# Mixer end of a two-layer hybrid block: the gate half of the last input chunk, the activation tables and the order of the output projection are rearranged

## The reference, cut to what matters

```
proj = h @ w_in ; rq, rk, rv, rg, sz, sxbc, sdt, bq, bk, bv = split(proj)
ro = head_groupnorm(retention(rq, rk, rv), w) * silu(rg)          # 256 columns
so = gated_rmsnorm(ssd(conv(sxbc), dt) + D*x, sz, w)               # 512 columns
bo = stick_breaking(bq, bk, bv)                                    # 256 columns
out = concat(ro, so, bo) @ w_out                                   # 1024 x 1024
```

## Time and profile before

| | before |
|---|---|
| median of 3 runs | 1516.62 us |
| lowest, highest | 1515.53, 1518.11 us |
| the profiled execution's own time | 1514.14 us |
| its span | 1512.0 us |
| PE busy | 1487.2 us (98%) |
| DVE busy | 1175.3 us (78%) |
| ACT busy | 981.7 us (65%) |

### The profile page before, as it was taken

One profiled execution on the slowest core, in us unless ns is written; L12 is line 12 of the kernel. 1 busy time (PEld: TensorE's weight loads), 2 busy tenths in 40 slices (PEclk: granted clock), 3 DMA queues, 4 the chain that ended last, 5 costly groups with the idle time before them and its releaser, 6 DMA issues.

```text
span 1512.0 us, 19204 instructions
## 1 busy us (share of the span) xinstructions
PE 1487.2 (98%) x7301; PEld 1237.0 (82%) x7304; DVE 1175.3 (78%) x844; ACT 981.7 (65%) x757; POOL 48.9 (3%) x53
## 2 busy tenths in 40 slices
PE   9999999999999999999999999999999999999997
PEld 7987788888988878888878888887888888888885
DVE  5875544444787698898878888878889888888886
ACT  6574533444556677777777777776777777777774
POOL 1010000000000000002000000200000200000010
PEclk9999999999999999999999999999999999999999
DMA  9625555554552499999989999999999998999992
GB/s 348 217 72 181 188 180 188 193 177 129 195 167 98 148 327 382 375 357 372 372 305 360 373 374 350 376 329 336 373 368 363 366 375 320 363 371 376 350 374 108
DMA packets 190647, 437.71 MB, mean 289 GB/s; under 512 B 9376, under 2 KB 13664, under 8 KB 190448
## 3 DMA queue, kind: packets, MB, share of 16 engines
q1 hardware_dynamic: 188256, 433.91, 80.0%
q0 software_dynamic: 1120, 2.20, 0.6%
q10 hardware_dynamic: 1200, 0.56, 0.1%
HBM read 435.59 MB, written 1.05 MB: 289 GB/s over the span
## 4 chain that ended last, share of the span: by engine, by line
PE 95%; DVE 3%; ACT 1%; issue 1%; DMA 0%; ACTq 0%; SPq 0%; DVEq 0%
PE ps L1316 29%; PE ps L1318 29%; PE ps L1317 29%; PE ps L1611 2%; PE ps L1568 1%; PE ps L1586 1%; PE ps L1587 0%; PE ps L1813 0%; PE ps L1379 0%; PE ps L1378 0%; PE ps L1377 0%; PE ps L1371 0%; DVE w_lo L831 0%; DMA x<-in_x_dram 0%; DVE hm L821 0%
## 5 line engine op out<-in xcount | busy, mean ns | idle before, releaser
L1163 DVE TENSOR_TENSOR w_lo<-raw,w_hi 128x2048 fp32r<-128x2048 f32 x333 | 754.6, 2289 | 122.5 <-ACT w_hi L658 120.0
L658 ACT ACTIVATE w_hi<-raw 128x2048 fp32r<-128x2048 f32 x332 | 630.2, 1919 | 170.5 <-PE ps L1318 170.5
L1316 PE MATMUL ps<-w_hi,aT_hi 128*128 128x512 f32 (+1 forms) x1296 | 511.0, 394 | 8.3 <-issue 3.2
L1318 PE MATMUL ps<-w_hi,aT_lo 128*128 128x512 f32 (+1 forms) x1296 | 503.4, 388 | 0.0
L1317 PE MATMUL ps<-w_lo,aT_hi 128*128 128x512 f32 (+1 forms) x1296 | 502.5, 388 | 0.0
L1316 PEld LDWEIGHTS ps<-w_hi,aT_hi 128*128 128x128 f32 x1296 | 243.4, 188 | 61.8 <-issue 5.9
L1318 PEld LDWEIGHTS ps<-w_hi,aT_lo 128*128 128x128 f32 x1296 | 243.2, 188 | 51.8
L1317 PEld LDWEIGHTS ps<-w_lo,aT_hi 128*128 128x128 f32 x1296 | 243.6, 188 | 48.6
L831 DVE TENSOR_TENSOR w_lo<-raw,w_hi 128x2048 fp32r<-128x2048 f32 (+2 forms) x81 | 176.7, 2186 | 101.8 <-ACT w_hi L478 101.6
L478 ACT ACTIVATE w_hi<-raw 128x2048 fp32r<-128x2048 f32 (+2 forms) x81 | 148.2, 1830 | 106.8 <-PE ps L1318 105.7
L1316 PE MATMUL ps<-w_hi,s2T_hi 128*128 128x512 f32 x544 | 213.1, 392 | 0.0
(11 more groups left out here) (274 smaller groups left out, 910.9 us busy)
## 6 DMA issues: line engine op xcount, KB each, us to landing
raw<-in_moe_w_gate_dram SPq DMA_DIRECT2D x112, 1024.0 KB, 6.9
raw<-in_moe_w_up_dram SPq DMA_DIRECT2D x112, 1024.0 KB, 7.6
raw<-in_moe_w_down_dram SPq DMA_DIRECT2D x112, 1024.0 KB, 7.0
raw<-in_w_in_dram SPq DMA_DIRECT2D x20, 1024.0 KB, 7.1
raw<-in_ffn_w_gate_dram SPq DMA_DIRECT2D x14, 1024.0 KB, 5.1
raw<-in_ffn_w_up_dram SPq DMA_DIRECT2D x14, 1024.0 KB, 5.1
raw<-in_ffn_w_down_dram SPq DMA_DIRECT2D x14, 1024.0 KB, 4.9
raw<-in_w_out_dram SPq DMA_DIRECT2D x8, 1024.0 KB, 5.1
```

The source lines that it names most:

```text
L658: nc.scalar.activation(moe_hi(pos), raw[:, slot, :], ACT.Copy).then_inc(hi_ready, 1)
L1163: V.tensor_tensor(moe_lo(pos), raw[:, pos % 6, :], moe_hi(pos).bitcast(F32), ALU.subtract)\
L1316: mm(out, lhs_hi, rhs_hi, start=start, stop=False, skip_group_check=True)
L1318: return mm(out, lhs_lo, rhs_hi, start=False, stop=stop, skip_group_check=True)
```

## The change

All of it is in the mixer, so it happens twice.

- Chunk 6 is no longer a `win_chunk`. `rvg_part(l, half, part)` multiplies 256 columns: part 0 is rv, for both token blocks into bank 1, and part 1 is rg into bank 0. The value part keeps the places of the two old halves. The gate part of both halves comes after the retention sums, and only it counts `split_used` up.
- ACT preloads one table that holds exp and ln ahead of abs, exp and ln, and again ahead of the last exp. It loads the sqrt table after the copy of rv and the silu table after the two square roots. The silu of rg and the split of piece 15 move behind the square roots, piece 15 first.
- Both `keep_warm` calls go. `mixT(0)` comes ahead of `log_weights`, into bank 3.
- `w_out` takes the steps 2, 3, 0, 1 of the first half, so it can begin with the quarter that `mixT(0)` brings. One block of `w_out(0, 1)` moves ahead of the weighted sums of stick breaking. The second half begins, for token block 0, with the steps 0 and 1 of both its pieces, ahead of the last quarter.
- On DVE the splits of pieces 15 and 16 each move one place forward.

```diff
-MIXT = [1, 0, 5, 4]
+MIXT = [1, 3, 5, 4]
 # ACT
+                nc.scalar.preload_act_table_set("natural_log_exp_and_others")
                 act.wait_ge(sb_z, l + 1)
...
-                chunk_done(6)
-                pv = ps[:, 0:2, :]
-                nc.scalar.activation(rv[:], pv[:, :, 0:256], ACT.Copy).then_inc(rv_ready, 1)
-                nc.scalar.activation(rg[:], pv[:, :, 256:512], ACT.Silu).then_inc(win_out, 1)
-                wout_split(l, 1)
+                both = lambda bank: ps[:, bank, :].rearrange("p (b n) -> p b n", b=NB)
+                act.wait_ge(rv_psum, l + 1)
+                nc.scalar.activation(rv[:], both(1), ACT.Copy).then_inc(rv_ready, 1)
+                sqrt_table()
...
+                nc.scalar.preload_act_table_set("silu_and_others")
+                wout_split(l, 1)
+                chunk_done(6)
+                nc.scalar.activation(rg[:], both(0), ACT.Silu).then_inc(rg_ready, 1)
...
                 mixT(1)
+                nc.scalar.preload_act_table_set("natural_log_exp_and_others")
                 wout_split(l, 2)
 # DVE
+                dve.wait_ge(rg_ready, l + 1)
                 V.tensor_tensor(hm[:, :, 0:256], cvf[:, 0:512].rearrange("p (b n) -> p b n", b=NB), rg[:], ALU.mult)\
...
                 mixT(0)
+                wout_split(l, 1)
                 mixT(1)
 
                 dve.wait_ge(sb_log, l + 1)
                 V.tensor_scalar(xb4, z4, 0.0, None, ALU.min).then_inc(sb_min, 1)
-                wout_split(l, 1)
+                wout_split(l, 2)
                 dve.wait_ge(sb_w, l + 1)
                 V.tensor_tensor(xb4, xb4, strict, ALU.mult).then_inc(sb_wm, 1)
-                wout_split(l, 2)
 # PE
+            def rvg_part(l, half, part):
+
+                g, bank, c0 = MIX_BASE[l] + 12 + half, (1, 0)[part], 256 * part
+                pe.wait_ge(lo_ready[g % 6], g // 6 + 1)
+                hi, lo = win_view(w_hi, g % SPL, 512), win_view(w_lo, g % SPL, 512)
+                for b in range(NB):
+                    for kk in range(4):
+                        k = 4 * half + kk
+                        ins = passes(ps[:, bank, b * 256:(b + 1) * 256], aT_hi[:, 2 * k + b, :], aT_lo[:, 2 * k + b, :],
+                                     hi[:, kk, c0:c0 + 256], lo[:, kk, c0:c0 + 256], start=k == 0 and b == 0,
+                                     stop=k == KD - 1)
+                return ins
...
-                win_chunk(l, 6, (0,))
+                rvg_part(l, 0, 0)
...
-                win_chunk(l, 6, (1,))
+                rvg_part(l, 1, 0).then_inc(rv_psum, 1)
...
                 ins.then_inc(ret_y, 1)
+                for half in range(2):
+                    rvg_part(l, half, 1).then_inc(split_used, 1)
...
+                pe.wait_ge(mix_ssd, l + 1)
+                mixT(0)
                 pe.wait_ge(sb_sp, l + 1)
                 for h in range(BH):
                     ins = log_weights(h)
                 ins.then_inc(sb_log, 1)
-                keep_warm(0, 8)
-                pe.wait_ge(mix_ssd, l + 1)
-                mixT(0)
                 pe.wait_ge(mix_ret, l + 1)
                 mixT(1)
-                keep_warm(2, 6)
+                pe.wait_ge(mixT_lo, 4 * l + 1)
+                w_out(0, 0, steps=(2, 3))
                 pe.wait_ge(mixT_lo, 4 * l + 2)
-                w_out(0, 0)
+                w_out(0, 0, steps=(0, 1))
+                w_out(0, 1, (0,))
                 pe.wait_ge(sb_wm, l + 1)
...
                 mixT(2)
-                w_out(0, 1, (0,))
+                w_out(0, 1, (1,))
                 pe.wait_ge(mix_sb, l + 1)
                 mixT(3)
-                w_out(0, 1, (1,))
+                pe.wait_ge(mixT_lo, 4 * l + 3)
+                w_out(1, 0, (0,), (0, 1))
+                w_out(1, 1, (0,), (0, 1))
                 pe.wait_ge(mixT_lo, 4 * l + 4)
-                w_out(1, 0, (0,))
-                w_out(1, 1, (0,))
-                w_out(1, 0, (1,))
+                w_out(1, 0, (0,), (2, 3))
+                w_out(1, 1, (0,), (2, 3))
+                w_out(1, 0, (1,), range(4))
```

More of the change, by code:

```diff
@@ L895, in mixer @@
                 dve.wait_ge(heads_in[l], 48)
-                dve.wait_ge(win_out, 7 * l + 1)
+                dve.wait_ge(win_out, 6 * l + 1)
                 V.tensor_tensor(sm3(2), sm3(2), bc(heads8[:, l, 0, :].unsqueeze(1), [P, NB, SH]), ALU.add)\
@@ L925, in conv @@
                     dve.wait_ge(conv_tap, taps[0])
-                dve.wait_ge(win_out, 7 * l + 2)
+                dve.wait_ge(win_out, 6 * l + 2)
                 conv(3, range(4))
@@ L933, in mixer @@
                 conv(0, range(4))
-                dve.wait_ge(win_out, 7 * l + 3)
+                dve.wait_ge(win_out, 6 * l + 3)
                 conv(3, range(4, XT))
@@ L939, in mixer @@
                 conv(0, range(4, XT))
-                dve.wait_ge(win_out, 7 * l + 4)
+                dve.wait_ge(win_out, 6 * l + 4)
                 dve.wait_ge(tables_in, 16)
@@ L1323, in win_chunk @@
                 if ci >= 2:
-                    pe.wait_ge(win_out, 7 * l + ci - 1)
+                    pe.wait_ge(win_out, 6 * l + ci - 1)
                 tiles = TILES_T.get(name, 0)
@@ L1425, in mixer @@
                 mm(cT[:, P:T], a3[:, 1], m_le, start=False, stop=True, **opts).then_inc(cs_psum, 1)
-                pe.wait_ge(win_out, 7 * l + 4)
+                pe.wait_ge(win_out, 6 * l + 4)
                 for m in range(4):
@@ L1461, in mixer @@
                 ins.then_inc(ret_psum, 1)
-                win_chunk(l, 6, (0,))
+                pe.wait_ge(win_out, 6 * l + 5)
+                rvg_part(l, 0, 0)
                 pe.wait_ge(s_ret, l + 1)
@@ L1467, in mixer @@
                 ins.then_inc(sb_z, 1)
-                win_chunk(l, 6, (1,))
-                pe.wait_ge(win_out, 7 * l + 6)
+                rvg_part(l, 1, 0).then_inc(rv_psum, 1)
+                pe.wait_ge(win_out, 6 * l + 6)
                 for g in range(SG):
@@ L1501, in mixT, with w_out @@
                     ins.then_inc(mixT_psum, 1)
-                def w_out(half, n, blocks=(0, 1), steps=range(4)):
+                def w_out(half, n, blocks=(0, 1), steps=(2, 3, 0, 1)):
                     g = MIX_BASE[l] + 14 + 2 * half + n
@@ L1510, in w_out @@
                             ins = passes(ps[:, 2 * b + n, :], aT_hi[:, 2 * k + b, :], aT_lo[:, 2 * k + b, :],
-                                         hi[:, kk, :], lo[:, kk, :], start=k == 0, stop=k == KD - 1)
-                        if (half, n, b) == (1, 1, 0):
+                                         hi[:, kk, :], lo[:, kk, :], start=k == 2, stop=k == KD - 1)
+                        if (half, n, b, steps[-1]) == (1, 1, 0, 3):
                             ins.then_inc(mix_block0, 1)
-                    if blocks[-1] == NB - 1 and steps[-1] == 3:
+                    if blocks[-1] == NB - 1 and steps[-1] == (1, 3)[half]:
                         ins.then_inc(split_used, 1)
+                pe.wait_ge(mix_ssd, l + 1)
+                mixT(0)
                 pe.wait_ge(sb_sp, l + 1)
@@ L1548, in mixer @@
                 else:
-                    w_out(1, 1, (1,))
+                    w_out(1, 1, (1,), range(4))
             def gather_fill(p, fill):
```

5 lines of the change are left out of this document (2 added, 3 removed).

## The result

The changed kernel takes 1511.92 us (median of 10 runs, 1508.69 to 1513.58) against 1516.64 us before (10 runs, 1514.19 to 1518.32). The ratio is 0.9965, 95% interval 0.9956 to 0.9974: by this ratio 5.3 us less, between 3.9 and 6.7 (the two medians are 4.7 apart). The forecast was 1510.1, 6.5 us less. The profiled executions took 1510.22 and 1514.14 us, with spans of 1508.1 and 1512.0.

What follows compares the result with a forecast made beforehand. PE was taken to bound the kernel. Per layer 4.76 - 0.75 - 0.10 - 0.65 = 3.26 us, twice 6.5, so 1516.6 - 6.5 = 1510.1 us; forecast's own range 1508.6 to 1511.6, wider range 1506.8 to 1514.0.

Steps and rivals of the forecast that it cites:

- The hole, 4.76 us: At each mixer end, PE's zero matmuls and waits before the first output projection would give way to real work, saving 4.76 us.
- The halved matmuls, +0.75: In the last input chunk, 96 matmuls of 256 columns instead of 48 of 512 would cost PE 0.75 us more per layer.
- The stick weights, +0.10: Ahead of the stick sums, PE would wait 0.1 us per layer for the stick weights, bounds 0 to 0.7.
- the tie: PE would ask for the stick weights at 114.1 us, just when their chain delivers them, 114.1 us.
- The wait for piece 17, +0.65: In the last output projection, PE would ask for piece 17 too early and newly wait 0.65 us per layer, bounds 0 and 1.4.
- Table loads bring nothing of their own: The table loads saved on ACT would gain no time, since ACT had idle time on both sides.
- The rival with a drain behind each load: ACT's table changes each cost 1.4 us more at the changed places, gain 3.3 us in all, 1513.3 us; a small chance.
- Slower halved matmuls: Weight loads no longer hide under 256 columns; at 0.19 us a matmul the run loses 7 us, 1523.6; chance 0.05 with other losses.
- The clock: Half clock on PE could appear at the mixer end or move in the router: 1.5 us either way, inside the forecast's range.

Runs made afterwards that it cites:

- e5: Kernel before, with only the last input chunk's 48 matmuls of 512 columns cut into 96 of 256, at the old places: 1519.50 us, ratio 1.0023.
- e2: Changed kernel, with piece 17 split on ACT and DVE before they turn to what waits for the stick sums: 1510.29 us, ratio 0.9961 to before.
- e3: Kernel before, with only the two preloads of the exp and ln table added: 1517.58 us, ratio 1.0003.
- e4: Kernel before, with only both groups of matmuls on zeros at the mixer end left out: 1521.49 us, ratio 1.0032.
- e11: Changed kernel, with its 20 opening zero matmuls written as 54 of 190 columns, 34 matmuls longer: 1510.41 us, ratio 0.9957 to before.
- e1: Changed kernel measured again without any edit, five rounds: 1511.42 us, ratio 0.9966 to before.
- e7: e2 with its 20 opening zero matmuls written as 54 of 190 columns, 34 matmuls longer: 1509.43 us, ratio 0.9955 to before.
- e12: Kernel before, with its 20 opening zero matmuls written as 96 of 107 columns, 76 matmuls longer: 1521.52 us, ratio 1.0032.
- e9: Kernel before, with its 20 opening zero matmuls written as 32 of 320 columns, 12 matmuls longer: 1516.56 us, ratio 0.9998.
- e10: Kernel before, with its 20 opening zero matmuls written as 24 of 426 columns, 4 matmuls longer: 1516.45 us, ratio 0.9993.
- e6: Kernel before, with its 20 opening zero matmuls written as 114 of 90 columns, 94 matmuls longer: 1518.29 us, ratio 1.0010.
- e8: e2 with 28 opening zero matmuls instead of 20: 1513.47 us, ratio 0.9987 to before.

## Why the prediction was nearly right

The mechanism came as forecast, at 3.18 and 3.19 us per mixer against 3.26. By its steps:

- *The hole, 4.76 us.* Right, by difference: with the other terms as measured it comes out at 3.18 + 0.64 + 0.12 + 0.78 = 4.72. The chain behind it was ready in time: no wait ahead of `mixT(1)` or the first projection.
- *The halved matmuls, +0.75.* Too large by 0.1. The new form took 3.07 + 2.98 + 5.84 = 11.89 us, forecast 11.91. But I had doubled the old second half, 5.58; the old first half, which follows the retention scores, took 5.67 (80.05 to 85.72). So it is +0.64; e5, with one start fewer, measured 0.56 and 0.52. The Trainium skill ("TensorE: Matmul & The Clock Gate", section "Back-to-back issue gap") gives columns over 2.4 GHz plus 2.5 ns as the gap of an isolated matmul, and says itself that this under-counts small ones in a stream with weight loads. The 0.1 us that I had estimated from it is too small here: starts were 0.120 us apart in the trace after too.
- *The stick weights, +0.10.* Right: the tie broke against PE by 0.39 us on the weight load, about 0.12 on the matmuls (0.35 from 115.63 to 115.98, where such a start takes 0.23).
- *The wait for piece 17, +0.65.* Right in place and cause, 0.78 in size, as e2 showed by removing it. The chain to it kept its 5.66 us from the end of the stick sums (118.71 to 122.08 + 2.29).
- *Table loads bring nothing of their own.* Right, e3. The rival with a drain behind each load is refuted: the silu's chain has a load of 1.28 us at 101.00, the next instruction at 102.30.
- *Slower halved matmuls.* Did not come, see above.
- *The clock.* At the mixer end it held. With nothing in the hole (e4) it did not, and the kernel took 4.9 us more in the median; in the profile 2.8 of 6.0 us lie at the mixer ends. The half-clock stretch at the start of the profiled execution, +1.79 us, is not the change's: a stretch like it, between 10 and 80 us, stands in 10 of the 14 profiles, in that of e5 too, which opens exactly as before does, and is missing in 4.
- *The step that failed* is one that I did not take: that stretches which no edit touches keep their length. I named another length of the expert stretch as a sign against me, and it came, +0.64 us in the profile and 1.0 to 1.2 in e1 and e2. The sum for this kernel is 6.4 from the mixers less 0.6 to 1.2; with the loop at a good place (e11) the median is 1510.41, which is the sum's 1510.1 within the runs' scatter.

That the second stall goes by the place of the loop in the program is shown by e7, e11 and e12, and by e5, e9 and e10, which have none. e6 does not belong here: its loss is the half clock. That PE waits for its own code is supported by the packet times above, though no run changed the fetching alone. The way out of the loop, at the third boundary between pairs, has no stall. Nor has the dense part's loop of 152 matmuls a round, against 1116 in the experts': PE never stood still for "issue" in it, and the instruction queue moved no packet from 181 to 383 us of the changed kernel. In e8 the same place cost 3.3 us more than in e12 because of the half clock behind both jumps and a longer second stall (3.31 us against 2.26). Where the costly band lies was not tried. An estimate: the next packet is of use some 5.0 us after PE starts again (774.07 to 779.03, 780.91 to 785.85), time for 22 matmuls of 0.227 us, so starts from +67 to +88 would be costly and +94 would not.

## What to carry to other kernels

A hole filled with matmuls on zeros is a place for real work, not for nothing: emptying it cost 4.9 us here (2.8 of the profile's 6.0 at the holes themselves), filling it won 6.4 in the two mixers. Work it out link by link, look for the piece that is now asked for too early, and move its preparation, in its engine's order, ahead of the wait for the end of the same stretch (another 1.6 us in the mixers). And when a change alters the number of instructions ahead of a hardware loop, compare the loop's own length in both traces before you judge the change, and read the granted clock in it, since a stretch at half clock looks like such a loss (e6). A few dozen harmless instructions more or fewer may give the loss back.

## What the hardware showed that was not expected

- The length of PE's program ahead of a loop changes the cost of the loop's backward jumps: the expert stretch was up to 4.6 us longer for two jumps, with the loop's own instructions and the clock the same (992.70 us before, 997.34 in e12), and 7.9 us longer in e8 with half clock behind both jumps. Eight more matmuls on zeros (e2 to e8) made the kernel 3.2 us slower in the median; 34 more made it faster (e7). Even at the best places a jump left PE 1.4 to 1.7 us without work. The short dense loop showed no such cost.
- The stretch at half clock in the first 80 us costs 1.5 to 1.9 us when it comes. Filling PE's idle time ahead of the first transposes (from 2.47 us in e2 to 0.70 in e8) did not remove it: both profiles have it at 74 to 76 us.
